# Two transformer blocks on one core: key rotation and two weight remainders moved from VectorE to GpSimd, one operand's scaling moved to ScalarE

## The reference

```
aq, ak, av, cq, bk, bv, bik, biw = split(h @ w_in)         # 512,128,128,256,64,64,64,8 columns
aq, ak = rope(aq), rope(ak)                                # 8 query heads, 2 key heads of 64
ya = sliding_window_attention_with_sinks(aq, ak, av)
cq = rms_norm(cq, q_norm)                                  # 256 wide
bq, biq = rope(cq @ w_uq), rope(cq @ w_uiq)                # second queries, index queries
bk, bik = rope(bk), rope(bik)                              # one key head each
yb = attention(bq, bk, bv) over the 64 best keys of relu(biq . bik) * iw
return concat(ya, yb) @ w_out
rope(t) = t * cos + concat(-t2, t1) * sin                  # t1, t2: the halves of a head
```

## Time and profile before

| | us |
|---|---|
| runs of the kernel | 1933.98, 1928.1, 1935.94 (median 1933.98) |
| the profiled execution | 1928.87 |
| its span, first to last instruction | 1927.0 |
| TensorE busy | 1826.0 (95%) |
| VectorE busy | 694.6 (36%) |
| ScalarE busy | 539.6 (28%) |
| GpSimd busy | 34.3 (2%) |

### The profile page before, as it was taken

The page is one execution under the profiler, slowest core; times in us unless marked ns, Lnnn a source line. Parts: engine busy times, 40 slices in busy tenths (PEclk is TensorE's granted clock), DMA queues, the critical chain, the costliest instruction groups (busy, mean ns, idle before and its releaser), DMA issues.

```text
span 1927.0 us, 24801 instructions
## 1 busy us (share of the span) xinstructions
PE 1826.0 (95%) x10198; PEld 1129.0 (59%) x10198; DVE 694.6 (36%) x1177; ACT 539.6 (28%) x714; POOL 34.3 (2%) x21
## 2 busy tenths in 40 slices
PE   6999989999999999999999999996899999989997
PEld 6785764443434434434434434464589987769996
DVE  3243322111111111111111111158865568676545
ACT  4342431101111111111111111045634454464442
POOL 0100120000000000000000000000000000000001
PEclk9998998999999999999999999997799999999999
DMA  9758599999999999999999999913144553424550
GB/s 337 285 197 329 187 380 398 428 428 429 428 428 429 429 429 428 429 428 429 428 428 429 429 429 428 418 59 119 32 165 175 190 213 142 175 103 143 202 197 34
DMA packets 96315, 587.14 MB, mean 305 GB/s; under 512 B 6990, under 2 KB 7204, under 8 KB 70660
## 3 DMA queue, kind: packets, MB, share of 16 engines
q1 hardware_dynamic: 94820, 581.25, 74.6%
q10 hardware_dynamic: 1440, 5.11, 0.8%
HBM read 585.30 MB, written 1.05 MB: 304 GB/s over the span
## 4 chain that ended last, share of the span: by engine, by line
PE 88%; DVE 4%; ACT 4%; DMA 3%; issue 1%; SPq 0%; DVEq 0%; ACTq 0%
PE bank L1063 34%; PE bank L1319 23%; PE bank L1338 12%; PE bank L1276 7%; PE bank L1348 3%; PE bank L1310 2%; DMA ring<-in_ada_w 1%; PE bank L1138 1%; ACT arena L811 1%; PE bank L1331 1%; PE bank L1123 1%; ACT sb_XN L896 1%; DMA ring<-in_w_o 1%; PE bank L1255 0%; DMA ring<-in_w_in 0%
## 5 line engine op out<-in xcount | busy, mean ns | idle before, releaser
L1319 PE MATMUL bank<-ring,arena 128*64 128x512 f32 x2048 | 454.7, 596 | 0.0
L1319 PEld LDWEIGHTS bank<-ring,arena 128*64 128x64 f32 x2048 | 141.6, 137 | 307.4 <-issue 307.4
L1063 PE MATMUL bank<-w_hi,arena_r 128*128 128x512 f32 (+1 forms) x784 | 258.0, 391 | 4.7 <-DVE arena_r L2027 2.8
L1338 PE MATMUL bank<-ring,arena 128*64 128x512 f32 x1024 | 226.8, 595 | 16.8 <-ACT arena L811 16.8
L502 DVE TENSOR_TENSOR w_lo<-ring,w_hi 128x4096 fp32r<-128x4096 f32 (+2 forms) x45 | 196.5, 4367 | 47.3 <-ACT w_hi L492 44.9
L1063 PEld LDWEIGHTS bank<-w_hi,arena_r 128*128 128x128 f32 x784 | 148.0, 189 | 35.4 <-DVE arena_r L2027 3.3
L492 ACT ACTIVATE w_hi<-ring 128x4096 fp32r<-128x4096 f32 (+2 forms) x45 | 158.9, 3574 | 34.9 <-DMA ring<-in_c_w_in 19.2
L809 ACT ACTIVATE arena<-arena,sb_tab 128x512 f32<-128x512 f32 x32 | 23.1, 722 | 510.5 <-DVE arena L1930 510.5
L1338 PEld LDWEIGHTS bank<-ring,arena 128*64 128x64 f32 x1024 | 72.5, 137 | 150.5 <-issue 144.9
L1905 DVE TENSOR_SCALAR arena<-sb_tab,sb_pos 128x64 f32<-128x64 f32 x66 | 13.8, 252 | 387.7 <-PE bank L1319 387.7
L1063 PE MATMUL bank<-XT_r,w_hi 128*128 128x256 f32 x512 | 145.8, 285 | 4.3 <-DVE arena_r L2148 4.3
(11 more groups left out here) (341 smaller groups left out, 2120.3 us busy)
## 6 DMA issues: line engine op xcount, KB each, us to landing
ring<-in_w_gate_up SPq DMA_DIRECT2D x128, 2048.0 KB, 14.4
ring<-in_w_down SPq DMA_DIRECT2D x64, 2048.0 KB, 16.7
ring<-in_mlp_w SPq DMA_DIRECT2D x32, 2048.0 KB, 8.3
ring<-in_ada_w SPq DMA_DIRECT2D x24, 2048.0 KB, 12.5
ring<-in_c_w_in SPq DMA_DIRECT2D x6, 2048.0 KB, 7.6
ring<-in_w_in SPq DMA_DIRECT2D x4, 2048.0 KB, 10.0
ring<-in_w_k SPq DMA_DIRECT2D x2, 2048.0 KB, 12.2
ring<-in_w_v SPq DMA_DIRECT2D x2, 2048.0 KB, 9.1
```

What stands on the lines that cost most here:

```text
L1063: mm = pe.matmul(out, st[a], mv[b], start=start and a + b == 0, stop=stop and a == 1, skip_group_check=True)
L1319: mm = pe.matmul(B[m][CAP * h:CAP * h + CAP, :], xe[:, 2 * j + kl, :], w[:, kl, m * D + h * HW:m * D + (h + 1) * HW], start=False, stop=(j ...
L1338: mm = pe.matmul(B[2][CAP * h:CAP * h + CAP, :], hT[:, c, CAP * j:CAP * j + CAP], w[:, c, h * HW:(h + 1) * HW], start=(j == 0 and c == 0), ...
```

## The change

GpSimd gets the rotation of ak, bk and bik (18 instructions, with waits for its own results where VectorE had them) and both `ab_out` remainders (two subtractions of 128x4096). Its temporary is another part of the tile XN than VectorE's. ScalarE scales the transposed cq, ahead of rounding `ab_out`. VectorE loses all of these. TensorE's and SyncE's programs stay as they are, and so do all semaphores that others wait for.

```diff
@@ gpsimd, after its four small operations on mod
+            pool_steps = [0]
+
+            def pool_link(ins):
+
+                pool_steps[0] += 1
+                ins.then_inc(sem("pool_step"), 1)
+                pool.wait_ge(sem("pool_step"), pool_steps[0])
+
+            pool.wait_ge(sem("rope_tables"), 1)
+            pool.wait_ge(sem("z0"), 3)
+            pool.wait_ge(sem("z1"), 3)
+            R1p = R1b.rearrange("p (t n) -> p t n", t=TB)
+            ptmp = XNf[:, 1536:1664].rearrange("p (g d) -> p g d", g=2)
+            for t in range(TB):
+                rope_on(pool, pool_link, R1p[:, t, 512:640].rearrange("p (g d) -> p g d", g=2),
+                        Z[:, t, 512:640].rearrange("p (g d) -> p g d", g=2), ptmp, t, None)
+                two = Z[:, t, 1024:1280 - 64].rearrange("p (m d) -> p m d", d=HD)[:, 0:3:2, :]
+                r2 = R2b[:, t, :].rearrange("p (m c d) -> p m c d", m=2, c=2)
+                rope_on(pool, pool_link, r2[:, :, 0, :], two, ptmp, t, None)
+                pool.tensor_copy(r2[:, :, 1, :], r2[:, :, 0, :]).then_inc(sem("k_rope"), 1)
+            split_lo(pool, "ab_out", 0)
+            split_lo(pool, "ab_out", 1)
             pool.wait_ge(*upto("ln3", "ln_landed", 32))
@@ scalar, behind the root of cq's squares
+            act.wait_ge(sem("ab_T"), 1)
+            for k in range(2):
+                act.activation(XTf[:, k * S:(k + 1) * S], B[6][:, k * S:(k + 1) * S], ACT.Copy,
+                               scale=gain("ab_q_norm_2")(k)).then_inc(sem("cqT"), 1)
             split_hi(act, "ab_out", 0)
             split_hi(act, "ab_out", 1)
@@ vector, behind the rotation of the first queries
             rope_aq(1)
-            dve.wait_ge(sem("ab_T"), 1)
-            for k in range(2):
-                dve.tensor_scalar(XTf[:, k * S:(k + 1) * S], B[6][:, k * S:(k + 1) * S], gain("ab_q_norm_2")(k), None,
-                                  ALU.mult).then_inc(sem("cqT"), 1)
-            for t in range(TB):
-                rope(R1a[:, t, 512:640].rearrange("p (g d) -> p g d", g=2),
-                     Z[:, t, 512:640].rearrange("p (g d) -> p g d", g=2),
-                     tmp[:, 0:128].rearrange("p (g d) -> p g d", g=2), t, None)
-                two = Z[:, t, 1024:1280 - 64].rearrange("p (m d) -> p m d", d=HD)[:, 0:3:2, :]
-                rope(R2b[:, t, :].rearrange("p (m c d) -> p m c d", m=2, c=2)[:, :, 0, :], two,
-                     tmp[:, 0:128].rearrange("p (g d) -> p g d", g=2), t, None)
-                r2 = R2b[:, t, :].rearrange("p (m c d) -> p m c d", m=2, c=2)
-                dve.tensor_copy(r2[:, :, 1, :], r2[:, :, 0, :]).then_inc(sem("k_rope"), 1)
             dve.wait_ge(sem("iq_mm"), 1)
@@ vector, ahead of the first scores
-            split_lo(dve, "ab_out", 0)
             for u in range(2):
                 front("ab", u, tb_("window"))
@@ vector, behind the attention
             gate_diag(0)
-            split_lo(dve, "ab_out", 1)
             split_lo(dve, "mlp0", 0)
```

## The result

| | kernel before | changed kernel |
|---|---|---|
| median of 17 runs | 1935.94 us | 1946.87 us |
| lowest, highest | 1928.1, 1942.84 | 1940.49, 1955.64 |
| ratio, 95% interval | | 1.0062 [1.0045, 1.0079] |
| span of the profiled execution | 1927.0 | 1940.9 |
| GpSimd busy | 34.3 us | 60.9 us |

The change costs 0.62% of 1935.94, 12.0 us, with an interval of 8.7 to 15.3 (the two medians lie 10.9 us apart). The changed kernel's lines from L660 on are numbered higher: the second queries' matmuls L1605 are now L1631, the transposes L1629 are L1655, the products L2213 are L2239, the score reduction L2043 is L2069. The kernels of the experiments shift the numbers again by a few lines.

What follows compares the result with a forecast made beforehand. TensorE bounds the kernel (88% of the span), with VectorE in the edited stretch's chain. The profiled execution's 1928.87 us + 14.5 of stops = 1943.4, or 1948.5 against the three-run median 1933.98; range 1937 to 1957.

Steps and rivals of the forecast that it cites:

- The wait, read from the earlier trace: Query rotations: VectorE sums with two SBUF inputs wait out GpSimd's two 9.0 us subtractions; +14.5 us.
- ended within a tenth of a GpSimd end: Sign in the changed profile: two VectorE L444 sums of 7 to 8 us end within a tenth of a GpSimd end.
- Rival 3: Query rotations: a long GpSimd subtraction lets a waiting VectorE sum in; +2.7 us, 1936.7; chance 0.15.
- GpSimd's keys end near 1305.86 + 6.8 + 4.5: Opening stretch: GpSimd's key work takes 6.8 us alone plus 4.5 of turns with VectorE, ending near 1317.1.
- if GpSimd wins the tie: At 1317.1: the sums of the first and second rotations wait instead, the fourth rotation ends at 1340.6; delay 15.2 us.
- (a): Second queries' operand evacuated by ScalarE instead of VectorE, ending near 1311.0 instead of 1312.39; gain 1.4 us.
- short turns: Opening stretch: L2213 waits for about two short GpSimd operations, making L1605 some 0.9 us late.
- (b): Four key rotations and two copies, 4.0 us, leave VectorE; they fill a wait for TensorE, worth 0.2 us.
- (c): Two subtractions of 128x4096, 4.43 us each, leave VectorE; both are hidden by TensorE's work, worth 0.
- GpSimd's prices: GpSimd: 2.17 ns a column and 0.14 us fixed; 0.43 us for 128 columns, 0.28 for 64, 9.0 for 4096.
- 1 (keys late): GpSimd's key rotations cost up to twice the flat price, keys at about 1324; +17.9 us, 1951.9; chance 0.10.
- 2 (does what it says): No harmful stops in the query rotations; the operand's 1.4 us is gained, 1932.6; chance 0.05.

Runs made afterwards that it cites:

- experiment 2: Kernel before with only the two ab_out remainders moved to GpSimd: ratio 1.0076 [1.0052, 1.01].
- experiment 3: Changed kernel with each of GpSimd's two subtractions of 4096 columns cut into eight of 512: ratio 0.9988 [0.9968, 1.0009] to the kernel before.
- experiment 1: Changed kernel with both ab_out remainders back on VectorE: ratio 0.9979 [0.9956, 1.0001] to the kernel before.
- experiment 7: Kernel before with only the operand's scaling moved to ScalarE: ratio 0.9988 [0.997, 1.0006].
- experiment 4: Changed kernel with only the first remainder on GpSimd, the second back on VectorE behind the attention: ratio 1.0015 [0.9995, 1.0035] to the kernel before.
- experiment 8: Changed kernel with GpSimd's first remainder behind VectorE's last rotation, the second on VectorE behind the attention: ratio 0.9983 [0.9967, 0.9999] to the kernel before.
- experiment 6: Changed kernel, both remainders back on VectorE, GpSimd subtracting an unused slot from itself twice: first query rotation to first score reduction 33.48 us (before 24.51), one run.
- experiment 9: Changed kernel, both remainders back on VectorE, three idle TensorE products in the wait for the last two rotations: ratio 0.9985 [0.9966, 1.0005] to the kernel before.
- experiment 10: As experiment 9, but GpSimd makes one remainder behind the last rotation in eight pieces of 512 columns: ratio 0.9973 [0.9955, 0.9991] to the kernel before.

## Why the prediction was right

Forecast 1948.5 us with 1937 to 1957; measured 1946.87. The mechanism is the one that was forecast, but part of the closeness is luck. The forecast is built on the median of three runs, 1933.98; over 17 runs the kernel before has 1935.94, and 14.5 us on top of that would have been 1950.4. By differences 14.5 us were forecast and 10.9 (medians), 12.0 (ratio) or 12.75 (stretch) measured. By its steps:

- **The wait, read from the earlier trace rows.** Right in kind and form. Two VectorE sums of 6.58 and 7.79 us ("7 to 8", the first just short of it), two stops for two instructions, the bank-fed products untouched. The sign "ended within a tenth of a GpSimd end" was mis-stated: they end some 0.55 us behind it, by the work that the prediction's own sum adds. That VectorE is held for the whole of a 9 us instruction, which only the Trainium skill (SBUF — State Buffer, Who interferes with whom) had stated, is now measured (8.84 and 8.83 us, experiment 2). Rival 3, which lets a waiting sum in, is refuted by these rows; experiment 3 shows what it takes to be let in, a boundary between instructions.
- **Size.** 14.5 us were forecast, 12.75 measured in the stretch, 12.0 in the ratio. The term that failed is the start of the first subtraction: "GpSimd's keys end near 1305.86 + 6.8 + 4.5", 11.2 us after the start. The first subtraction began after 9.3 (1303.40 to 1312.73). The turns with VectorE were taken to cost GpSimd 4.5 us on top of its own 6.8. An undisturbed rotation took 1.61 us in the changed profile (1310.87 to 1312.48) and a copy 0.25 to the next start, so four rotations and two copies come to 7.0, and the turns cost 2.3. That the two engines' work overlapped in part is read from the rows only; no run isolates it. The branch was the second of the two ("if GpSimd wins the tie", first and second rotation stopped), forecast at 15.2: less 1.9 for the earlier start and 0.5 for two subtractions that took 18.09 us where 18.6 with a turn were assumed, this gives 12.8, against 12.75 measured in the stretch. The first subtraction even ran for 2.8 us (1312.73 to 1315.57) before a sum was asked for.
- **(a), the operand on ScalarE,** 1.4 us; measured alone 1.33. In the change, short turns were to take back 0.9; experiment 1 shows L1605 5.43 us after the first rotation against 5.25 in experiment 7, so they took 0.2. The two products L2213 took 0.80 us instead of 0.62, not 0.9 more. Same mis-sizing as above.
- **(b), the keys,** worth 0.2: experiment 7 keeps them on VectorE and has the same stretch as experiment 1, which does not, to 0.2 us. **(c), the remainders,** worth 0: both experiments keep these on VectorE, so they say nothing of it, but the changed kernel does. Its first score reduction starts 5.07 us behind the end of the last rotation without a remainder between them, that of the kernel before 4.94 us with one. The work moved away was covered by waits for TensorE.
- **GpSimd's prices.** 9.0 us for 4096 columns: 8.82 to 8.87 where nothing held it (changed kernel, experiments 2, 4 and 8), and 18.09 for two with the turn between them. 0.43 and 0.28 us: 0.46 and 0.32 undisturbed; the copy 0.29 for 0.3.
- **The clock.** Not foreseen: in the changed profile L1605 took 8.68 us instead of 7.13, its clock granted at 0.84 in 1310 to 1316. It took as long in experiments 2, 3 and 6 (8.83, 8.80 and 8.76 us) and 7.13 in all others; why was not looked for. In the changed kernel it did not matter, since the first sum only waited less.

```profile
1308.83 8.68 PE L1631 MATMUL bank<-ring,XT 128*128 128x512 f32 x16 [0.93 <-ACT XT L963]
```

- **Rivals.** 1 (keys late): out, they were early. 2 (does what it says): its 1.4 us gain exists, but only without the remainders.
- **Chances.** 0.74 for slower by over 0.5%: the ratio is 0.62%, its interval reaches down to 0.45%, and by the medians alone it is 0.56%, so the case was as near the mark as the text said.

## What to carry to other kernels

Before work is moved to GpSimd because it is idle, list what VectorE does at that time by its operands. An operation with two SBUF inputs stopped here for the rest of a GpSimd instruction that reads SBUF (8.84 us at most), and a tensor-scalar operation from SBUF to SBUF also beside one that only writes (3.53 us). Operations fed from PSUM with one SBUF input kept their 0.69 and 0.41 us. So put GpSimd's work beside PSUM-fed work, and cut it into pieces no longer than a wait that VectorE can afford. And look for such rows in the trace at hand: here one 1.34 us record among 0.69 us ones at the kernel's end priced a change in its middle.

## What the runs showed of the hardware that was not expected

- A VectorE tensor-scalar of 128x8, 0.17 us by itself, took 8.69 us beside a GpSimd subtraction and 3.53 beside a fill that reads nothing; the smallest operations can be the ones that stop.
- A GpSimd subtraction of a slot from itself took 7.0 and 7.3 us for 4096 columns (14.43 for two), one of two different tiles with an fp32r result 8.8 to 8.9.
- The scatter between executions of the same kernel goes with TensorE's mean granted clock over the whole span. Of 30 runs of the kernel before, the fastest took 1927.33 us at a mean of 0.980, the slowest 1943.63 at 0.970; the changed kernel's 17 go from 1940.49 at 0.978 to 1955.64 at 0.967. That is 1.4 to 1.6 us for each 0.001. Which of the two makes the other was not tested. The scatter is larger than this edit's 12 us, so a single pair of runs can hide it.
- Three idle products in a wait of 2.6 us held the granted clock of the next ten microseconds at 0.98 in the profiled execution of experiment 9 (and 1.00 in that of experiment 10, 1322 to 1332 us) instead of 0.50.
